# Two mixer stacks on one core: softmax sums spread by TensorE, convolution taps moved later, rotations issued inside a projection

## The chip, the core and the metric

The kernel runs on one core of one Trainium2 chip. The metric is the device time of one execution in microseconds; it is read as the median of several runs. All rows are from one profiled execution of the kernel before.

## What is computed

Input x has 256 positions of 1024 features. The first stack has two layers; each is an RMS norm, a projection `w_in` to 14 groups of 256 columns, four branches, and a projection `w_out` added to x. Two branches are attentions over 4 heads of 64: a sliding window with a sink logit (c) and a neighbourhood attention with a learned bias (d). Each needs

```
p = softmax(scores)           # per head and query, 256 keys
y = (p @ v) * silu(z)         # z: the branch's gate
```

Branch a is a 31-tap depthwise convolution, then a layer norm and SiLU; branch b a gated 3-tap convolution. The second stack has two layers of feed-forward, mixer, feed-forward; its mixer has two causal attentions, one of them (dilated, `dq`, `dk`, `dv`) with a partial rotary embedding of q and k, and a gated linear recurrence computed in 7 levels. Everything is float32. Weights and activations are split into a rounded part and a remainder, so that each product is three matmuls (hi·hi, hi·lo, lo·hi).

## The kernel before

The order of work is written by hand, engine by engine, and tied by semaphores. A mixer is a row of **slots**: slots 0 to 13 are the 14 column groups of `w_in` (orders `ORDER_1`, `ORDER_2`), 14 to 17 the four row groups of `w_out`. A slot is one 1 MB weight tile in a ring of three: SP loads it, ScalarE (ACT) rounds it into `w_hi` (L511), VectorE (DVE) subtracts into `w_lo` (L937), TensorE (PE) multiplies (`project`, 16 steps of 3 matmuls, L1660 to L1662), and DVE or ACT copies the sum out of PSUM (`copy_out`, L990). `project` takes a table `between`: work issued ahead of one of its 16 steps.

An attention is four units (2 branches by 2 blocks of 128 queries). Unit u of the first stack runs so:

- end of PE slot 7+u: `scores` (L1787); DVE in its slot 7+u: `soft` adds the mask or bias and takes the row maximum; ACT: `softmax_exp` with the row sums.
- DVE slot 8+u, first thing: `finish` inverts the sums (L1017) and scales heads 0 and 1 (L1021); ACT slot 8+u: `normalize` scales heads 2 and 3 (L583).
- PE slot 9+u, ahead of step 7 (`TURN_AT`): `turn_probs` transposes the probabilities (L1800), after waiting for both halves of the scaling; ACT copies them to SBUF (`pt_copy`, L613); end of PE slot 9+u: `values` (L1811), then `scores` of unit u+2; DVE: `gated_y` multiplies the result by the gate (L1148).

The second stack's units run the same way, but there ACT scales all heads and `plain_y` takes the result.

DVE also computes the first 20 taps of channel half 0 of the convolution (L1135), in the slots of `DVE_TAPS_AT`; POOL adds the other taps' products, which ACT makes, adds the two parts (L1571), and then does the short convolution of branch b. PE transposes the sum in slot 14 (`conv_to_tm`, L1889), ahead of its second block.

In slots 7 and 8 of the second stack, after the scores, PE multiplies `dq` and `dk` by the rotation matrix into the PSUM tile `aux` (L2036), and DVE's `rotate` (L1031 to L1036) reads it. `aux` is a single tile that the levels of the recurrence (`packed_tile` L1968, read by `take_level` L1357) use too; its users take turns in the order `AUX_ORDER_2`.

```
DVE_TAPS_AT = {2: 3, 3: 3, 4: 2, 5: 2, 6: 2, 8: 2, 9: 2, 10: 2, 11: 2}
TURN_AT = 7
LEVEL_AT = [2 * KT, 2 * KT - 1, 2 * KT - 2, ...]   # level lv goes ahead of step 16-lv of slot 6+lv
```

Of the kernel before, what the change touches and what calls it, by code (L numbers as in the profile page):

```python
# [15 lines left out]
P = 128  # L16
D = 1024
S = 256
# [32 lines left out]
for _i, _n in enumerate(["hq0", "hq1", "hf0", "hf1", "hi0", "hi1", "hg0", "hg1"]):  # L51
# [15 lines left out]
DVE_TAPS_AT = {2: 3, 3: 3, 4: 2, 5: 2, 6: 2, 8: 2, 9: 2, 10: 2, 11: 2}  # L67
# [96 lines left out]
def stacks_kernel(nc, a, out):  # L164

    with ExitStack() as ctx:
# [153 lines left out]
        inv_ready, scaled_dve, scaled_act = sem("inv_ready"), sem("scaled_dve"), sem("scaled_act")  # L320
# [172 lines left out]
        def _(act):  # L493
# [83 lines left out]
            def normalize(un, u, heads, keys=S):  # L577
# [3 lines left out]
                for h in heads:  # L581
                    pr = probs[:, u % 2, h * S:h * S + keys]
                    ins = nc.scalar.activation(pr, pr, ACT.Copy, scale=row_inv[:, c + h:c + h + 1])  # L583
                ins.then_inc(scaled_act, 1)
# [87 lines left out]
            for l in range(DEPTH):  # L672
                base, base3, un = l * LAYER_1, l * (LAYER_1 // RING), l * 4
                gates = 0
                for i, name in enumerate(ORDER_1):
# [5 lines left out]
                    if SC_1 + 1 <= i < SC_1 + 5:  # L681
                        normalize(un, i - SC_1 - 1, (2, 3))
# [20 lines left out]
                    if i == 12:  # L703
# [53 lines left out]
            for l in range(DEPTH):  # L757
# [87 lines left out]
                for i, name in enumerate(ORDER_2):  # L845
# [12 lines left out]
                    if SC_2 + 1 <= i < SC_2 + 5:  # L858
                        normalize(un, i - SC_2 - 1, range(NH), causal_keys(i - SC_2 - 1))
# [58 lines left out]
        def _(dve):  # L918
# [93 lines left out]
            def finish(un, u, has_sink):  # L1012
# [6 lines left out]
                for h in range(2) if un < DEPTH * 4 else ():  # L1019
                    pr = probs[:, u % 2, h * S:(h + 1) * S]  # L1020
                    ins = v.tensor_scalar(pr, pr, row_inv[:, c + h:c + h + 1], None, ALU.mult)  # L1021
                    if h:
                        ins.then_inc(scaled_dve, 1)
# [92 lines left out]
            for l in range(DEPTH):  # L1116
# [25 lines left out]
                def gated_y(u, kt):  # L1142

                    g = proj[:, ix["c_z"] if u < 2 else ix["d_z"], :].rearrange(two, s=S)
                    cols = slice((u % 2) * P, (u % 2 + 1) * P)
                    yv = y_f[:, 0:2 * P].rearrange("p (c s) -> p c s", s=P)
                    dve.wait_ge(mix_written, un + u + 2)
                    v.scalar_tensor_tensor(out=yv, in0=mix[:, 0:2 * P].rearrange("p (c s) -> p c s", s=P), scalar=0.5,  # L1148
                                           in1=g[:, :, cols], op0=ALU.mult, op1=ALU.mult).then_inc(mix_read, 1)
# [4 lines left out]
                for i, name in enumerate(ORDER_1):  # L1154
                    if i == 0:
                        dve.wait_ge(rb_ready, l + 1)
                    if 0 <= i - SC_1 - 1 < 4:
                        finish(un, i - SC_1 - 1, i - SC_1 - 1 < 2)
# [17 lines left out]
                    u = i - SC_1  # L1176
# [937 lines left out]
```

## Time and profile before

| | us |
|---|---|
| median of 3 runs (1280.44 to 1281.99) | 1281.68 |
| the profiled execution, own time | 1284.26 |
| its span in the trace | 1282.4 |
| PE busy / DVE busy / ACT busy / POOL busy | 1261.0 / 987.5 / 705.3 / 262.1 |

The span is the time between the first and the last recorded instruction; the execution's own time has 1.9 us more (1284.26-1282.4). A row of the timeline gives start, duration, engine, line, output<-inputs and count; "[x <-Y]" behind it is idle time just before the row and the work whose end released it. Matmul durations include a drain that overlaps the next matmul, so the pace is read from start to start.

### The profile page before, as it was taken

Reading aid. Unit: us, or ns where it says so; the run is one execution under the profiler, and the core shown is the slowest. Engines: PE = TensorE matmul, PEld = TensorE weight load, DVE = VectorE, ACT = ScalarE, POOL = GpSimd, SP = SyncE. Lnnn points to the kernel's source line nnn. Section 1 sums busy time; section 2 is a strip of 40 time slices with the busy share of each in tenths; the row PEclk is TensorE's granted clock in tenths of the full one; section 3 lists DMA queues with packets and bytes.
Section 4 is the critical chain, followed back from the end, with each engine's and each line's share of the span. In section 5 each row is a group of like instructions: output and inputs, shape, how many; then the busy total and the mean of one; then the engine's idle time right before and its main releaser. Section 6 shows DMA issues by size and latency. Waiting matters only on the chain.

```text
span 1282.4 us, 20996 instructions
## 1 busy us (share of the span) xinstructions
PE 1261.0 (98%) x7922; PEld 1123.4 (88%) x7922; DVE 987.5 (77%) x1195; ACT 705.3 (55%) x945; POOL 262.1 (20%) x258
## 2 busy tenths in 40 slices
PE   9989999999999999999999999999999999999998
PEld 8978998888888899988888888888889998888886
DVE  5998789889766769777776678777676976876676
ACT  5775567465444587736444445444458683644444
POOL 2753164375000023201000009200011320100000
PEclk9999999999999999999999999999999999999999
DMA  8963653556666545346666655766654535666661
GB/s 266 259 186 134 205 157 132 174 171 199 194 196 196 165 133 164 110 128 190 197 197 196 190 170 165 206 188 196 196 158 139 165 107 160 178 197 195 185 187 55
DMA packets 281358, 224.00 MB, mean 175 GB/s; under 512 B 25996, under 2 KB 264234, under 8 KB 281288
## 3 DMA queue, kind: packets, MB, share of 16 engines
q1 hardware_dynamic: 279144, 220.23, 57.1%
q10 hardware_dynamic: 2032, 2.67, 0.7%
q8 instruction: 46, 0.75, 0.3%
q14 instruction: 24, 0.20, 0.0%
q0 software_dynamic: 112, 0.15, 0.0%
HBM read 221.85 MB, written 3.14 MB: 175 GB/s over the span
## 4 chain that ended last, share of the span: by engine, by line
PE 80%; DVE 13%; issue 2%; ACT 2%; DMA 1%; SPq 1%; POOLq 0%; DVEq 0%; POOL 0%; ACTq 0%
PE wide L1693 25%; PE wide L1696 13%; PE big L1660 8%; PE big L1661 8%; PE big L1662 8%; DVE w_lo L937 4%; PE wide L1660 4%; PE wide L1661 4%; PE wide L1662 4%; PE big L1717 1%; DVE work L1135 1%; DVE probs L1000 1%; DMA w_raw<-in_w_in 1%; DVE proj L990 1%; DVE small L1005 1%
## 5 line engine op out<-in xcount | busy, mean ns | idle before, releaser
L937 DVE TENSOR_TENSOR w_lo<-w_raw,w_hi 128x2048 fp32r<-128x2048 f32 x203 | 472.8, 2332 | 96.8 <-ACT w_hi L511 92.3
L511 ACT ACTIVATE w_hi<-w_raw 128x2048 fp32r<-128x2048 f32 x204 | 389.8, 1912 | 163.8 <-PE big L1662 126.5
L1693 PE MATMUL wide<-h_both,w_hi 128*128 128x512 f32 x1408 | 356.7, 393 | 0.0
L1693 PEld LDWEIGHTS wide<-h_both,w_hi 128*128 128x128 f32 x1408 | 254.5, 189 | 48.6 <-DVE h_both L952 2.0
L1660 PE MATMUL wide<-h_both,w_hi 128*128 128x256 f32 x736 | 213.8, 291 | 0.0
L1661 PE MATMUL wide<-h_both,w_hi 128*128 128x256 f32 x736 | 208.1, 283 | 0.0
L1662 PE MATMUL wide<-h_both,w_lo 128*128 128x256 f32 x736 | 208.0, 283 | 0.0
L1696 PEld LDWEIGHTS wide<-h_both,w_lo 128*128 128x128 f32 x1408 | 194.2, 190 | 15.0
L1696 PE MATMUL wide<-h_both,w_lo 128*128 128x256 f32 x1408 | 198.8, 282 | 0.0
L1660 PE MATMUL big<-w_hi,y_hi 128*128 128x512 f32 x480 | 189.1, 394 | 0.0
L1661 PE MATMUL big<-w_lo,y_hi 128*128 128x512 f32 x480 | 187.3, 390 | 0.0
L1662 PE MATMUL big<-w_hi,y_lo 128*128 128x512 f32 x480 | 187.0, 390 | 0.0
L727 ACT ACTIVATE work<-wide 128x512 f32<-128x512 f32 x88 | 52.5, 597 | 234.0 <-PE wide L1696 233.9
L1660 PEld LDWEIGHTS wide<-h_both,w_hi 128*128 128x128 f32 x736 | 140.9, 191 | 5.5 <-issue 4.2
L1661 PEld LDWEIGHTS wide<-h_both,w_hi 128*128 128x128 f32 x736 | 141.0, 192 | 0.6 <-issue 0.5
L1662 PEld LDWEIGHTS wide<-h_both,w_lo 128*128 128x128 f32 x736 | 140.9, 191 | 0.0
L1528 POOL TENSOR_SCALAR small<-small 128x1 f32<-128x1 f32 (+1 forms) x20 | 4.5, 223 | 601.2 <-ACT probs L515 551.2
L1251 DVE TENSOR_TENSOR work<-wide,work 128x512 f32<-128x512 f32 x88 | 60.7, 690 | 85.0 <-ACT work L727 85.0
L1662 PEld LDWEIGHTS big<-w_hi,y_lo 128*128 128x128 f32 x480 | 90.1, 188 | 19.3
L1660 PEld LDWEIGHTS big<-w_hi,y_hi 128*128 128x128 f32 x480 | 90.3, 188 | 17.0
L1661 PEld LDWEIGHTS big<-w_lo,y_hi 128*128 128x128 f32 x480 | 90.4, 188 | 16.6
L1556 POOL TENSOR_TENSOR work<-work,fz 128x256 f32<-128x256 f32 x60 | 64.4, 1073 | 27.1 <-ACT fz L597 23.0
(252 smaller groups left out, 1461.6 us busy)
## 6 DMA issues: line engine op xcount, KB each, us to landing
w_raw<-in_w_in SPq DMA_DIRECT2D x112, 512.0 KB, 4.8
w_raw<-in_ffn_w_gate SPq DMA_DIRECT2D x88, 512.0 KB, 4.0
w_raw<-in_ffn_w_up SPq DMA_DIRECT2D x88, 512.0 KB, 5.2
w_raw<-in_ffn_w_down SPq DMA_DIRECT2D x88, 512.0 KB, 4.2
w_raw<-in_w_out SPq DMA_DIRECT2D x32, 512.0 KB, 4.0
work<-rpb_shifted SPq DMA_DIRECT2D x32, 64.0 KB, 3.3
rpb_shifted<-rpb_rows SPq DMA_DIRECT2D x10, 147.0 KB
x<-in_x SPq DMA_DIRECT2D x2, 512.0 KB, 6.7
```

Source lines behind the costliest of these rows:

```text
L511: nc.scalar.activation(w_hi[:, r, :], w_raw[:, r, :], ACT.Copy).then_inc(hi_ready, 1)
L727: nc.scalar.activation(tmp_cross[parity].rearrange("p (c s) -> p c s", s=S), wide[:, 2 * parity:2 * parity + 2, S:2 * S], ACT.Copy).then_i ...
L937: v.tensor_tensor(w_lo[:, r, :], w_raw[:, r, :], w_hi[:, r, :].bitcast(F32), ALU.subtract).then_inc(lo_ready, 1)
L990: ins = v.tensor_tensor(proj[:, i, :].rearrange(view, s=S), pj[:, i % 2, :].rearrange(view, s=S), row_scale[:].unsqueeze(1).to_broadcast([ ...
L1000: ins = v.scalar_tensor_tensor(out=pr, in0=big[:, 0:2, :].rearrange("p a (h k) -> p (a h) k", k=S)[:, :, 0:keys], scalar=SCALE, in1=bias, ...
L1251: v.tensor_tensor(both, wide[:, 2 * parity:2 * parity + 2, 0:S], tmp_cross[parity].rearrange(view, s=S), ALU.add).then_inc(pj_read[parity], 1)
L1556: g.tensor_tensor(acc, acc, fz[:, n % PROD_RING, :], ALU.add).then_inc(prod_used, 1)
L1660: t_.matmul(o, a_hi, b_hi, start=first, stop=False, skip_group_check=True)
L1661: t_.matmul(o, a_hi, b_lo, start=False, stop=False, skip_group_check=True)
L1662: return t_.matmul(o, a_lo, b_hi, start=False, stop=last, skip_group_check=True)
L1693: t_.matmul(o, hi[:, kt, c], h_both[:, kt].rearrange("p a s -> p (a s)"), start=kt == 0, stop=False, skip_group_check=True)
L1696: ins = t_.matmul(o[:, 0:S], lo[:, kt, c], h_hi[:, kt, :], start=False, stop=kt == KT - 1, skip_group_check=True)
```

## The change

Three edits. In the first stack the probabilities are turned unscaled: `turn_probs` waits for the exponentials only, the scaling on DVE (L1021) and ACT (L583) is gone, and a new `spread_inverse` on PE broadcasts the inverse sums over the 64 rows of each head into `aux`, at the end of slots 9 to 12; `gated_y` multiplies gate by spread sums and then by the values. `finish` goes behind `copy_out` and stands behind that in the same slot. The turn was already inside a projection and stays there.

The six taps that DVE did in slots 8, 9 and 10 go to slot 6 (three taps instead of two), 11 (three instead of two) and 12 (four instead of none); 20 in all as before. ACT makes the short convolution's products one slot earlier (11), and POOL's addition of the two parts goes behind the short convolution's additions.

In the second stack each rotation goes from behind the scores of slot 7 or 8 to ahead of step 4 of slot 8 or 9, and so ahead of that slot's level in the order of `aux`.

```diff
-DVE_TAPS_AT = {2: 3, 3: 3, 4: 2, 5: 2, 6: 2, 8: 2, 9: 2, 10: 2, 11: 2}
+DVE_TAPS_AT = {2: 3, 3: 3, 4: 2, 5: 2, 6: 3, 11: 3, 12: 4}
-AUX_1 = 4
+AUX_1 = 8
 TURN_AT = 7
+ROT_AT = 4
...
-               + [f"{kind}{i}" for i in range(6, 13) for kind in ("level", "turn")
-                  if kind == "level" or i in (7, 8)]
+               + [f"{kind}{i}" for i in range(6, 13) for kind in ("turn", "level")
+                  if kind == "level" or i in (8, 9)]
...
-                    if SC_1 + 1 <= i < SC_1 + 5:
-                        normalize(un, i - SC_1 - 1, (2, 3))
...
-                    if i == 12:
+                    if i == 11:
                         short_products(l)
...
-                for h in range(2) if un < DEPTH * 4 else ():
-                    pr = probs[:, u % 2, h * S:(h + 1) * S]
-                    ins = v.tensor_scalar(pr, pr, row_inv[:, c + h:c + h + 1], None, ALU.mult)
...
+                    dve.wait_ge(aux_written, n + 1)
+                    v.scalar_tensor_tensor(out=scaled_gate, in0=aux[:, 0:2 * P].rearrange("p (c s) -> p c s", s=P), scalar=0.5,
+                                           in1=g[:, :, cols], op0=ALU.mult, op1=ALU.mult).then_inc(aux_read, 1)
+                    dve.wait_ge(aux_read, n + 2)
                     dve.wait_ge(mix_written, un + u + 2)
-                    v.scalar_tensor_tensor(out=yv, in0=mix[:, 0:2 * P].rearrange("p (c s) -> p c s", s=P), scalar=0.5,
-                                           in1=g[:, :, cols], op0=ALU.mult, op1=ALU.mult).then_inc(mix_read, 1)
+                    v.tensor_tensor(yv, mix[:, 0:2 * P].rearrange("p (c s) -> p c s", s=P), scaled_gate, ALU.mult
+                                    ).then_inc(mix_read, 1)
...
+            def spread_inverse(n, u, order=HORDER):
+                pe.wait_ge(inv_ready, n + 1)
+                for c in range(2):
+                    for low in range(2):
+                        at = 4 * (u % 2) + order[2 * c + low]
+                        ins = t_.matmul(aux[low * HD:(low + 1) * HD, c * P:(c + 1) * P],
+                                        row_inv[:, at:at + 1].to_broadcast([P, HD]), ident, start=True, stop=True,
+                                        skip_group_check=True)
+                ins.then_inc(aux_written, 1)
...
+                    if 0 <= u - 2 < 4:
+                        aux_free()
+                        spread_inverse(l * 4 + u - 2, u - 2, PLAIN if u - 2 < 2 else HORDER)
...
+                    if i in (8, 9):
+                        between[ROT_AT] = rotation
```

PE, first stack, end of slot 9 of layer 0, before (L1811 are the values of unit 0, L1787 the scores of unit 2, L1660 begins slot 10):

```order
L1811 MATMUL wide<-pT,proj 64x128 [waits mix_read,pt_read,cv_ready]
L1811 MATMUL wide<-pT,proj 64x128 x7
L1787 MATMUL big<-proj 128x256 [waits sc_read]
L1787 MATMUL big<-proj 128x256 x3
L1660 MATMUL wide<-h_both,w_hi 128x256 [waits pj_read_even,lo_ready]
```

and with the change (line numbers of the changed file):

```order
L1811 MATMUL wide<-pT,proj 64x128 [waits mix_read,pt_read,cv_ready]
L1811 MATMUL wide<-pT,proj 64x128 x7
L1786 MATMUL big<-proj 128x256 [waits sc_read]
L1786 MATMUL big<-proj 128x256 x3
L1820 MATMUL wide<-cst,small 64x128 [waits inv_ready,aux_read]
L1820 MATMUL wide<-cst,small 64x128 x3
L1659 MATMUL wide<-h_both,w_hi 128x256 [waits pj_read_even,lo_ready]
```

Four matmuls (L1820) stand ahead of the next projection, with a wait for `finish` and one for the tile `aux`.

DVE, first stack, slot 12 of layer 0, before:

```order
L990 TENSOR_TENSOR proj<-wide,row_scale 128x512 [waits slot_done]
L1148 SCALAR_TENSOR_TENSOR y_f<-wide,proj 128x256 [waits mix_written]
L944 CAST y_hi<-y_f 128x2x128 [waits mix_read]
L945 TENSOR_TENSOR y_lo<-y_f,y_hi 128x2x128 [waits dve_chain]
L937 TENSOR_TENSOR w_lo<-w_raw,w_hi 128x2048 [waits hi_ready,yd_ready]
```

and with the change:

```order
L989 TENSOR_TENSOR proj<-wide,row_scale 128x512 [waits slot_done]
L1144 SCALAR_TENSOR_TENSOR tmp<-wide,proj 128x256 [waits aux_written]
L1148 TENSOR_TENSOR y_f<-wide,tmp 128x256 [waits mix_written,aux_read]
L943 CAST y_hi<-y_f 128x2x128 [waits mix_read]
L944 TENSOR_TENSOR y_lo<-y_f,y_hi 128x2x128 [waits dve_chain]
L1129 SCALAR_TENSOR_TENSOR work<-work,parA_all 128x256 [waits yd_ready]
L1129 SCALAR_TENSOR_TENSOR work<-work,parA_all 128x256 [waits dve_chain] x3
L936 TENSOR_TENSOR w_lo<-w_raw,w_hi 128x2048 [waits dve_chain,hi_ready]
```

The gate is multiplied in two steps, and the last four taps (L1129) now stand here, ahead of the remainder of slot 15's weights.

PE, second stack, end of slot 7 of the first mixer, before (L2036 is the rotation of `dq`):

```order
L1787 MATMUL big<-proj 128x128 [waits sc_read,foxc_ready]
L1787 MATMUL big<-proj 128x128 x3
L1790 MATMUL big<-y_lo,y_hi 128x128 x4
L2036 MATMUL wide<-proj,cst 128x256 [waits pj_read_even,aux_read]
L2036 MATMUL wide<-proj,cst 128x256
L1660 MATMUL wide<-w_hi,h_both 128x256 [waits pj_read_even,lo_ready]
```

and with the change:

```order
L1786 MATMUL big<-proj 128x128 [waits sc_read,foxc_ready]
L1786 MATMUL big<-proj 128x128 x3
L1789 MATMUL big<-y_lo,y_hi 128x128 x4
L1659 MATMUL wide<-w_hi,h_both 128x256 [waits pj_read_even,lo_ready]
...
L1661 MATMUL wide<-w_hi,h_both 128x256
L2020 MATMUL wide<-proj,cst 128x256 [waits pj_read_even,aux_read]
L2020 MATMUL wide<-proj,cst 128x256
L1659 MATMUL wide<-w_hi,h_both 128x256
```

Twelve matmuls of slot 8 (left out here but for the first and the last) now run ahead of the rotation and of its wait for `aux`.

## Rows read from the trace of the kernel before

**Rows 1.** The page: busy times; the chain that ended last, by engine.
```profile
PE 1261.0 (98%) x7922; PEld 1123.4 (88%) x7922; DVE 987.5 (77%) x1195; ACT 705.3 (55%) x945; POOL 262.1 (20%) x258
...
PE 80%; DVE 13%; issue 2%; ACT 2%; DMA 1%; SPq 1%; POOLq 0%; DVEq 0%; POOL 0%; ACTq 0%
```

**Rows 2.** The waits of PE over the span: us in total, times, longest.
```profile
PE big L1800 <- ACT probs L583: 9.6, 8, 2.9
PE wide L2036 <- DVE at_x L1357: 3.3, 4, 1.2
```

**Rows 3.** Busy time by stretch: slots 9 and 10, first layer; first number the length.
```profile
67.50:79.50 12.00, 9.10 (x81) 8.22 (x81) 11.60 (x14) 8.14 (x20) 8.01 (x8) 1.00 0.79 229
79.50:89.40 9.90, 9.08 (x82) 8.20 (x80) 9.48 (x15) 6.68 (x15) 3.35 (x5) 1.00 0.59 199
```

**Rows 4.** Timeline of PE: slot 9 of layer 0.
```profile
73.15 1.09 PE L1800 MATMUL big<-cst,probs 128*128 128x128 f32 x8 [2.90 <-ACT probs L583]
74.00 0.36 PE L1660 MATMUL wide<-h_both,w_hi 128*128 128x256 f32 x1
...
77.39 1.09 PE L1811 MATMUL wide<-pT,proj 128*64 128x128 f32 x16
78.42 1.14 PE L1787 MATMUL big<-proj 64*128 64x256 f32 x8
```

**Rows 5.** Timeline, slots 6 to 9 of layer 0; last row slot 7 of layer 1.
```profile
58.74 1.82 DVE L1135 SCALAR_TENSOR_TENSOR work<-work,parA_all 128x256 f32<-128x256 f32 x2
...
64.57 5.58 DVE L937 TENSOR_TENSOR w_lo<-w_raw,w_hi 128x2048 fp32r<-128x2048 f32 x2
...
71.32 0.56 DVE L1016 TENSOR_TENSOR small<-small 128x4 f32<-128x4 f32 x1
...
72.78 0.68 DVE L990 TENSOR_TENSOR proj<-wide,row_scale 128x512 f32<-128x512 f32 x1
...
67.47 0.39 PE L1660 MATMUL wide<-h_both,w_hi 128*128 128x256 f32 x1
...
74.83 1.00 ACT L613 ACTIVATE pT<-big 128x1024 f32<-128x1024 f32 x1
...
186.25 0.69 DVE L990 TENSOR_TENSOR proj<-wide,row_scale 128x512 f32<-128x512 f32 x1 [2.39 <-PE wide L1662]
```

**Rows 6.** Timeline of PE: inverse roots spread over 128 rows, and the matmul behind.
```profile
146.58 0.60 PE L1725 MATMUL big<-cst,small 128*128 128x128 f32 x4
146.94 0.36 PE L1660 MATMUL wide<-h_both,w_hi 128*128 128x256 f32 x1
```

**Rows 7.** Timeline, layer 0, slots 11 to 14: DVE, POOL, PE.
```profile
103.66 1.01 DVE L1135 SCALAR_TENSOR_TENSOR work<-work,parA_all 128x256 f32<-128x256 f32 x2
...
107.62 0.41 DVE L1148 SCALAR_TENSOR_TENSOR y_f<-wide,proj 128x256 f32<-128x256 f32 x1
108.06 1.03 DVE L944 CAST y_hi<-y_f 128x256 fp32r<-128x256 f32 x1
...
104.89 2.81 POOL L1571 TENSOR_TENSOR work<-work,part_sum 128x256 f32<-128x256 f32 x1 [7.49 <-DVEq L1191]
...
110.04 5.23 POOL L1556 TENSOR_TENSOR proj<-proj,fz 128x256 f32<-128x256 f32 x4 [1.09 <-ACT fz L597]
...
106.45 1.09 PE L1811 MATMUL wide<-pT,proj 128*64 128x128 f32 x16
...
114.72 0.60 PE L1889 MATMUL wide<-cst,work 128*128 128x128 f32 x4
```

**Rows 8.** Timeline, second stack, first mixer, slots 8 and 9: PE, then DVE.
```profile
513.67 1.13 PE L2036 MATMUL wide<-proj,cst 128*128 128x256 f32 x4 [1.22 <-DVE at_x L1357]
514.45 0.47 PE L1660 MATMUL wide<-w_hi,h_both 128*128 128x256 f32 x1
...
507.61 0.68 DVE L1031 TENSOR_TENSOR tmp<-wide,sin 128x512 f32<-128x512 f32 x1
...
512.89 0.73 DVE L1357 COPY_PREDICATED at_x<-masks,wide 128x512 f32<-128x512 uint8 x1
```

More of the change, by code:

```diff
@@ L575, in softmax_exp, with normalize @@
                 ins.then_inc(probs_exp, 1)
-            def normalize(un, u, heads, keys=S):
+            def normalize(un, u, keys):
                 act.wait_ge(inv_ready, un + u + 1)
                 c = 4 * (u % 2)
-                for h in heads:
+                for h in range(NH):
                     pr = probs[:, u % 2, h * S:h * S + keys]
                     ins = nc.scalar.activation(pr, pr, ACT.Copy, scale=row_inv[:, c + h:c + h + 1])
-                ins.then_inc(scaled_act, 1)
+                ins.then_inc(probs_scaled, 1)
             def tap_products(l, k0, k1):
@@ L858, in _ @@
                     if SC_2 + 1 <= i < SC_2 + 5:
-                        normalize(un, i - SC_2 - 1, range(NH), causal_keys(i - SC_2 - 1))
+                        normalize(un, i - SC_2 - 1, causal_keys(i - SC_2 - 1))
                     if i != 3:
@@ L1176, in _ @@
                     u = i - SC_1
+                    if 0 <= u - 1 < 4:
+                        finish(un, u - 1, u - 1 < 2)
                     if 0 <= u < 4:
@@ L1455, in _ @@
                         q = proj[:, ix["dq" if i == 7 else "dk"], :]
-                        rotate(ax2 + AUX_IX_2[f"turn{i}"], q, cos2[:], sin2[:], 2, q)
+                        rotate(ax2 + AUX_IX_2[f"turn{i + 1}"], q, cos2[:], sin2[:], 2, q)
                     if 0 <= u - 2 < 4:
@@ L1568, in _ @@
                     add_product(l * PRODS + k - 1, conv_acc[:, c] if c else part)
-                pool.wait_ge(conv_part, l + 1)
-                pool.sem_inc(pool_step, 1)
-                g.tensor_tensor(conv_acc[:, 0], conv_acc[:, 0], part, ALU.add).then_inc(conv_ready, 1)
                 two = "p (c s) -> p c s"
@@ L1583, in _ @@
                         add_product(l * PRODS + TAP_PRODS + 2 * c + j - 1, cbx[:, c])
+                pool.wait_ge(conv_part, l + 1)
+                pool.sem_inc(pool_step, 1)
+                g.tensor_tensor(conv_acc[:, 0], conv_acc[:, 0], part, ALU.add).then_inc(conv_ready, 1)
                 pool.wait_ge(*evacuated(l * NPROJ + ORDER_1.index("b_b")))
@@ L1794, in turn_probs @@
             def turn_probs(n, u, keys=S):
-                pe.wait_ge(scaled_act, n + 1)
                 if n < DEPTH * 4:
-                    pe.wait_ge(scaled_dve, n + 1)
+                    pe.wait_ge(probs_exp, n + 1)
+                else:
+                    pe.wait_ge(probs_scaled, n - DEPTH * 4 + 1)
                 pe.wait_ge(pt_read, n + 1)
@@ L1997, in _, with turn_unit, rotation @@
                         between = {FLIP_AT: turn_second, CROSS_AT: cross} if pl == LEVELS else {}
+                    def turn_unit():
+                        turn_probs(l * 4 + 8 + i - SC_2 - 2, i - SC_2 - 2, causal_keys(i - SC_2 - 2))
+                    def rotation():
+                        aux_free(f"turn{i}")
+                        src = ix["dq" if i == 8 else "dk"]
+                        pe.wait_ge(*evacuated(mq + src))
+                        for c in range(2):
+                            ins = t_.matmul(aux[:, c * S:(c + 1) * S], rot2, proj[:, src, c * S:(c + 1) * S],
+                                            start=True, stop=True)
+                        ins.then_inc(aux_written, 1)
+                    if i in (8, 9):
+                        between[ROT_AT] = rotation
                     if 0 <= i - SC_2 - 2 < 4:
-                        between[TURN_AT] = lambda: turn_probs(l * 4 + 8 + i - SC_2 - 2, i - SC_2 - 2, causal_keys(i - SC_2 - 2))
+                        between[TURN_AT] = turn_unit
                     if i >= 2:
@@ L2030, in _ @@
                                    causal_keys(u))
-                    if i in (7, 8):
-                        aux_free(f"turn{i}")
-                        src = ix["dq" if i == 7 else "dk"]
-                        pe.wait_ge(*evacuated(mq + src))
-                        for c in range(2):
-                            ins = t_.matmul(aux[:, c * S:(c + 1) * S], rot2, proj[:, src, c * S:(c + 1) * S],
-                                            start=True, stop=True)
-                        ins.then_inc(aux_written, 1)
                 def hgrn_out(t):
```

8 lines of the change are left out of this document (3 added, 5 removed).

## Prediction

> **What bounds the kernel now.** I read the page's busy times and the chain that ended last first: PE is busy for 98% of the span and holds 80% of the chain [rows 1]. So work that leaves DVE or ACT is worth nothing by itself; only PE's own work and PE's waits count. The view of PE's waits names them. The turns of the first stack wait 9.6 us in eight places for the scaled probabilities, the longest 2.9; the rotations of the second stack wait 3.3 us in four places for a level to be read out of the shared tile, the longest 1.2 [rows 2]. The rest of PE's waits stand at the start of the kernel. Third, the stretches: in slot 9 of layer 0 DVE is busy 11.60 of 12.00 us, in slot 10 9.48 of 9.90, while PE's own work is 9.1 in both [rows 3]. Here alone DVE sets the pace, and PE's waits are what is left over. Fourth, the timeline, to see what each wait would meet next.
>
> Changes within 0.2% (2.6 us) count as no change here, about what a measurement can tell.
>
> **Turns without the scaling.** The eight waits go if nothing else is late. The turn then needs the exponentials, which the slot before has finished: for unit 0 they are followed only by the scaling that leaves. Gain 9.6 us. The scaling itself (two operations on DVE, two on ACT per unit) runs beside PE and counts nothing once the wait is gone; the second step in `gated_y` adds one operation like the 0.41 us one [rows 7] in its place, also beside PE.
>
> **The spread of the sums.** Per unit four matmuls of 128 columns with 64-wide weights, all on PE's path. The nearest row has this shape: the values are eight such matmuls, recorded as 16, and take 78.42-77.39 = 1.03 us from start to start [rows 4], so four take 0.51. The other near row spreads inverse roots by the same trick, but over 128 rows: two matmuls take 146.94-146.58 = 0.36 us [rows 6], so four would take 0.72. I take 0.51, since halves of 64 rows alternate as in the values; 8 x 0.51 = 4.1 us, bounds 4.1 and 5.8. This is a cost on the very engine that bounds. The Trainium skill ("FP8 and Floating Point Precision", TensorE Precision Notes) says that true FP32 goes through the array in four passes; by that alone a unit would cost 4 x 4 x 128 columns at 2.4 GHz, an estimate of 0.85 us, or 6.8 us in all. The values are the same kind of matmul at 0.13 us each [rows 4], less than the 0.21 of four passes, so the rule and the trace differ, and the row decides for the cheaper price.
> Its waits: the inverse sums come out of DVE a slot earlier, right behind `copy_out`. For unit 0 `copy_out` ends at 72.9 (below), the inverse some 0.8 us later, and PE wants them behind the values and the scores, at 77.4. The tile was read in the slot before. No wait.
>
> **One more tap in slot 6.** In layer 0 DVE runs without a gap from the two taps at 58.74 to the double remainder at 64.57, whose first half ends at 64.57+5.58/2 = 67.4; PE starts slot 9, which needs it, at 67.47 [rows 5]. A third tap (1.82/2 = 0.91) makes this start 0.9 us later, at 68.4. In layer 1 DVE idles 2.39 us before its slot 7 [rows 5], and the tap is free. Cost 0.9 us. What is late next is ACT's copy of the turned probabilities, which stands behind a tanh that waits for DVE's `copy_out` of slot 8. That moves by +0.91 for the tap and by 72.78-71.32 = 1.46 the other way, since `finish` and the scaling no longer stand ahead of it; the copy ends at 74.83+1.00-0.55 = 75.3 [rows 5]. PE reaches the values 21 matmuls of (77.39-74.00)/27 = 0.126 and then 77.39-73.15 = 4.24 us [rows 4] after 68.4, at 75.3. They meet; 0.1 us at most.
>
> **Taps out of slots 8 to 10.** Two taps take 1.8 us [rows 5]. With them and the scaling (0.6) gone and one operation of 0.41 [rows 7] added, DVE's slot 10 falls from 9.48 [rows 3] to 7.5, below PE's 9.1+0.5 with the spread. This is what keeps the waits from coming back elsewhere.
>
> **Last taps in slot 12.** PE's `conv_to_tm` needs POOL's final addition. Now that is ready 7 us before it is wanted (104.89+2.81 against 114.72) [rows 7]. With the change DVE does `gated_y` behind the spread of slot 12 (2.2 us: two operations of 0.41, the cast and a remainder, with the links between), then four taps at 0.5 (1.01/2) = 2.0, then POOL 0.1+2.8, because a weight remainder starts beside it as now. That is 7.2 us after the spread; PE gets from the start of slot 13 (106.45+1.03) to `conv_to_tm` in 114.72-107.48 = 7.2 us [rows 4, 7]. They meet as well. Each layer: 0.15 us; bounds 0, if the addition takes the 1.1 us of an undisturbed one, and 1.6, if the taps go at 0.91 [rows 5]. POOL's short additions, now ahead, take 5.2 us and start one slot (9 us) before 110.04 [rows 7], so they end some 2 us before the last tap. Cost 0.3 us.
>
> **Rotations inside the projection.** The wait at 513.67 ends with DVE's reading of the level, 512.89+0.73 = 513.62 [rows 8]. DVE has no gap in this stretch, so it does not get earlier. PE does: without this wait and the first rotation's (3.3/2-1.22 = 0.4) it starts slot 9 at 513.67-1.22-0.4 = 512.0 and reaches step 4, twelve matmuls on, at 513.4, so some 0.25 us of wait are left. In slot 8 the level now follows the rotation in the tile: DVE reads the rotation by 507.61+0.68 = 508.3 [rows 8], PE wants the tile at 508.5. It just passes. Against this, leaving a projection once more costs: behind scores, the next projection's second matmul is 0.1 us late. Gain per mixer 3.3/2-0.25-2x0.1 = 1.2 us, in all 2.4; bounds 0 and 3.3. DVE's `rotate` waits for PE now, but PE passes step 4 before DVE is through `soft`, so DVE stands still for nobody. Behind `rotate` wait the next `finish` and remainder; two slots of slack.
>
> **Sum.** -9.6+4.1+0.9+0.3 = -4.3 in the first stack, -2.4 in the second: 6.7 us less. The profiled execution's own 1284.26 would become 1277.6; it stands 2.6 above the median of the runs, 1281.68, so for the median I say 1281.68-6.7 = **1275.0**.
>
> **Rivals.**
> 1. *The convolution tail binds.* If the last taps take 0.9 each, PE waits 1.6 in each layer, 3.2 instead of 0.3: 1277.9. For it: taps do cost that while POOL works [rows 5]. Against: POOL should be idle by then.
> 2. *The spread does not run in pairs.* At 0.72 each 1.7 us more, 1276.7. For it: the rows of the other spread. Against: its weights are 128 wide, these are 64. By the four passes that the Trainium skill names, full and one after another, it would be 1277.7 (an estimate).
> 3. *Rotations keep their wait.* PE meets DVE at the tile a little further on (at level 8, where I have 0.2 us of margin), and the second stack gives nothing: 1277.4.
> 4. *The first stack gives nothing back.* PE's waits move from the turn to the values, which need ACT's copy; DVE, not PE, still paces slots 9 to 12. Then only the second stack gains: about 1279.5, no change.
> 5. *Slower.* The spread is a new wait on PE, in order ahead of every projection, and `gated_y` must have read the tile and the values before the next ones. If DVE's slot took over 1.2 us more than PE's 9.6, that is 10.8, PE would lose 1.2 us at each of eight spreads, 9.6 in all, against 6.7: 1284.6. For it: the cast in `gated_y` takes 1.03 instead of 0.3 us when POOL works beside it [rows 7], and one operation was added. Against: I count 7.5 us for DVE's slot, so 3.3 would have to come from somewhere. That decides against it.
> That the change does not do what it says can be excluded: the order of instructions shows each move.
>
> **Chances.** Forecast 0.56, rival 1 0.12, rival 2 0.08, rival 3 0.12, rival 4 0.08, slower 0.04. Rivals 1 to 3 are still faster by over 2.6 us: faster 0.87, same 0.09, slower 0.04 ("same" is rival 4 and 0.01 for rivals 1 and 3 together). The range: at best every wait goes, 9.6+3.3-4.1 = 8.8 us, which gives 1272.9; less half the spread of the runs shown (0.8) and something for waits that cost more than their idle time: 1271.5. At the other end rivals 1 to 3 and part of rival 4: 1279.5.
>
> **What would show it.** In the profile after: no wait of PE before the turns, or under 0.3 us; eight records per spread, 0.51 us from start to start; slot 9 of layer 0 starting at 68.3 instead of 67.5; `conv_to_tm` starting within 0.5 us of the end of POOL's addition, with a wait of PE under 0.4; one wait of about 0.25 us before the second rotation of each mixer. A wait of PE before L1811, before L1820 or before the projections of slots 10 to 13 would make the prediction wrong, as would taps of 0.9 us in slot 12.

## The result and the profile after

| | before | changed |
|---|---|---|
| median of 4 runs each (lowest to highest) | 1281.12 us (1280.44 to 1281.99) | **1272.19 us** (1271.64 to 1273.19) |
| ratio (95% interval) | 1 | 0.993 (0.9914 to 0.9945), 8.9 us less |
| span of the profiled execution | 1282.4 | 1269.8 |

Three more comparisons of the changed kernel, made beside the experiments below, gave 1272.52, 1271.69 and 1272.02 us, ratios 0.9926, 0.9925 and 0.993. So the change is worth 9 to 10 us. ("us less" is worked out from the ratio here and below, so it can differ by some tenths from the difference of two medians.) The forecast was 6.7 us less (1275.0); the time lies in its range, 2.8 us below the number.

The page of the changed kernel, its busy times and the chain that ended last, beside [rows 1]:

```profile
PE 1260.5 (99%) x7986; PEld 1124.0 (89%) x7986; DVE 986.7 (78%) x1187; ACT 697.5 (55%) x929; POOL 270.0 (21%) x258
...
PE 90%; DVE 6%; ACT 2%; issue 2%; DMA 0%; POOLq 0%; SPq 0%; DVEq 0%; POOL 0%; ACTq 0%
```

PE's busy time is about the same, 1260.5 against 1261.0 us, although 64 records were added: the profiled execution of before also has two stretches in which PE ran at half its pace (below), so this line does not show what the spread costs. PE's share of the chain rose from 80% to 90%, DVE's fell from 13% to 6%. The waits of PE, whole list, in the columns of [rows 2]:

```profile
PE wide L1832 <- DVE kc L1036: 1.5, 1, 1.5
PE big L1716 <- DMA x<-in_x: 1.1, 1, 1.1
PE wide L1659 <- DVE h_both L951: 0.3, 1, 0.3
```

All three stand in the first 10 us. No turn and no rotation has a mark of idle time any more; both rows of [rows 2] are gone. PE in slots 9 and 10 of layer 0, the answer to [rows 4]; unit 2, without scores behind its values, stands under the first dots:

```profile
73.00 1.09 PE L1811 MATMUL wide<-pT,proj 128*64 128x128 f32 x16
74.03 1.13 PE L1786 MATMUL big<-proj 64*128 64x256 f32 x8
75.09 0.66 PE L1820 MATMUL wide<-cst,small 128*64 128x128 f32 x8
75.68 0.38 PE L1659 MATMUL wide<-h_both,w_hi 128*128 128x256 f32 x1
...
91.98 1.09 PE L1811 MATMUL wide<-pT,proj 128*64 128x128 f32 x16
92.90 0.61 PE L1820 MATMUL wide<-cst,small 128*64 128x128 f32 x8
93.44 0.39 PE L1659 MATMUL wide<-h_both,w_hi 128*128 128x256 f32 x1
```

The spread L1820 takes 0.59 us from start to start behind scores and 0.54 behind values. The values in front of it give some back when the spread follows them: 92.90-91.98 = 0.92 instead of 1.03. So it adds 0.59 in units 0 and 1 and 0.43 in units 2 and 3, 4.1 us over the kernel.

The same two slots by stretch, in the columns of [rows 3]:

```profile
66.20:75.68 9.48, 9.48 (x90) 8.63 (x89) 9.09 (x10) 6.72 (x18) 7.67 (x7) 1.00 0.96 282
75.68:85.17 9.49, 9.49 (x91) 8.64 (x89) 9.01 (x12) 8.40 (x16) 4.83 (x6) 1.00 0.63 215
```

PE is busy from end to end. A slot takes 9.48 us where it took 12.0 and 9.9. DVE, the third pair, still has 9.0 of 9.5 us of work, not the 7.5 that I had counted.

**One yardstick for all kernels.** The inverse-root spread (L1725 before, L1724 after, [rows 6]) opens each stage of a layer. From its first start to its second is layer 0 of the first stack with its FFN, to its third is layer 1; the fourth to the fifth and the seventh to the eighth hold one mixer of the second stack each. The start-up and what happens elsewhere drop out of these differences (us):

| kernel | layer 0 | layer 1 | mixer 1 | mixer 2 |
|---|---|---|---|---|
| before | 126.74 | 125.03 | 136.00 | 137.48 |
| changed | 122.46 | 122.35 | 134.56 | 134.51 |
| e1 rotations only | 125.53 | 125.06 | 134.54 | 134.50 |
| e2 taps only | 124.09 | 123.87 | 135.99 | 135.92 |
| e3 spread only | 122.70 | 122.70 | 136.00 | 137.46 |
| e4 early finish, no spread | 125.06 | 123.41 | 134.59 | 134.51 |
| e5 spread and rotations | 122.47 | 122.68 | 134.58 | 134.50 |
| e6 spread twice | 123.94 | 124.16 | 134.62 | 134.51 |
| e7 six taps in slot 6 | 123.78 | 122.36 | 134.61 | 134.52 |
| e9 wide spread | 126.98 | 130.45 | 134.58 | 134.47 |
| e11 wide copy | 123.80 | 124.20 | 134.55 | 134.48 |

The differences between before and changed are 4.28, 2.68, 1.44 and 2.97, in all 11.4 us. Another 1.2 lie at the start, so the spans differ by 12.6, more than the medians' 8.9. Three parts of that belong to the one profiled execution of before. At the start the same eight transposes took longer in it (before, then changed), and its matmuls kept that slower pace until 10.5 us, though the profile gives a granted clock of 1.00 there:

```profile
6.92 1.94 PE L1717 MATMUL big<-cst,x 128*128 128x128 f32 x8 [0.81 <-DMA x<-in_x]
...
6.81 1.07 PE L1716 MATMUL big<-cst,x 128*128 128x128 f32 x8 [1.09 <-DMA x<-in_x]
```

Its layer 0 is 1.2 us longer than that of e1, which runs the same first stack. And the 1.5 us more in its mixer 2 are lost clock: behind the wait of the second rotation, whose row in mixer 1 [rows 8] has 1.13 us of busy time, PE was granted half its clock, 1.2 instead of 2.4 GHz. The rotation, then the stretch behind it (granted clock: third number from the end):

```profile
1020.32 1.76 PE L2036 MATMUL wide<-proj,cst 128*128 128x256 f32 x4 [1.20 <-DVE at_x L1357]
...
1020.80:1024.10 3.30, 3.30 (x15) 3.03 (x14) 3.26 (x6) 0.43 (x1) 0.00 (x0) 0.50 0.94 294
```

Matmuls of 256 columns start every 0.21 us there instead of every 0.12. e3, with its rotations unchanged, shows the same behind its wait of 1.21 (137.46, granted clock 0.50 from 1013.4 to 1016.6 us); e2, with the same wait of 1.22, does not. The changed kernel has no such stretch before its last few microseconds in any of its four profiles. Against e1 for the first stack and e2 for the mixers, the change gives 3.07+2.71+1.43+1.41 = 8.6 us, near the medians' 8.9. Lost clock also spreads the runs of before: of those made beside the experiments the two slowest, 1285.07 and 1284.89 us, had mean granted clocks of 0.994 and 0.995, the two at 1.000 took 1280.67 and 1280.66, and all of the change's lie at 0.999 or 1.000.

### The profile page after: what moved, and what is told of

It reads as the page before. It is cut to its first block, busy times and chain, and to the rows that moved or that the text cites. A ratio compares the mean times of both kernels' runs of the same rounds, so it can differ in the third digit from the quotient of the medians.

```text
span 1269.8 us, 21116 instructions
## 1 busy us (share of the span) xinstructions
PE 1260.5 (99%) x7986; PEld 1124.0 (89%) x7986; DVE 986.7 (78%) x1187; ACT 697.5 (55%) x929; POOL 270.0 (21%) x258
## 4 chain that ended last, share of the span: by engine, by line
PE 90%; DVE 6%; ACT 2%; issue 2%; DMA 0%; POOLq 0%; SPq 0%; DVEq 0%; POOL 0%; ACTq 0%
PE wide L1692 26%; PE wide L1695 13%; PE big L1659 9%; PE big L1660 9%; PE big L1661 8%; PE wide L1659 6%; PE wide L1660 6%; PE wide L1661 6%; DVE w_lo L936 2%; PE wide L1811 1%; PE big L1716 1%; PE big L1800 1%; PE big L1786 1%; DVE work L1345 1%; PE wide L1981 1%
## 5 line engine op out<-in xcount | busy, mean ns | idle before, releaser
L1660 PE MATMUL wide<-h_both,w_hi 128*128 128x256 f32 x736 | 208.1, 283 | 0.0
L1660 PE MATMUL big<-w_lo,y_hi 128*128 128x512 f32 x480 | 187.3, 390 | 0.0
L1660 PEld LDWEIGHTS wide<-h_both,w_hi 128*128 128x128 f32 x736 | 141.0, 192 | 0.5 <-issue 0.5
L1660 PEld LDWEIGHTS big<-w_lo,y_hi 128*128 128x128 f32 x480 | 90.4, 188 | 16.6
```

What stands on the lines that cost most here:

```text
L1660: t_.matmul(o, a_hi, b_lo, start=False, stop=False, skip_group_check=True)
```

## Experiments

Every kernel ran beside the kernel before on the same chip. "Change" is the changed kernel, and lines of edits are named as in the diff.

**The parts apart: e1, e2, e3.** e1 takes the hunks on the rotations alone (`AUX_ORDER_2`, `ROT_AT`, `rotation()`, `turn{i + 1}`); e3 those on the sums' path (`AUX_1`, the semaphores, `normalize`, `finish`, `gated_y`, `turn_probs`, `spread_inverse`); e2 the taps and what goes with them, POOL's last addition moved behind its short ones and:

```diff
-DVE_TAPS_AT = {2: 3, 3: 3, 4: 2, 5: 2, 6: 2, 8: 2, 9: 2, 10: 2, 11: 2}
+DVE_TAPS_AT = {2: 3, 3: 3, 4: 2, 5: 2, 6: 3, 11: 3, 12: 4}
-                    if i == 12:
+                    if i == 11:
                         short_products(l)
```

> Only the rotations go inside the projections of slots 8 and 9; the first stack stays as before. My theory (each edit takes away its own wait of PE, and the three add up): 2 x 1.42 us, as the two traces show it for the first mixer, so 2.8 us less than the kernel before, and no wait of PE before the rotations. Rival (PE meets DVE at the shared tile a little later, and the gain of the whole change came from the first stack): within 1 us of before, with a wait before the level or the second rotation.

Measured: 1278.03 us against 1281.74, ratio 0.9973 (0.9961 to 0.9984), 3.5 us less. The yardstick says 1.4 us per mixer.

> Only the taps of slots 8 to 10 move to slots 6, 11 and 12, with POOL's final addition behind the short convolution; the scaling of the probabilities stays and nothing is spread. Theory A (the scaling is what PE waits for, so only the spread takes the waits away): the eight waits before the turns stay within 1 us of their 9.6 in sum, time within 1 us of before. Theory B (DVE's queue is what makes the scaling late, and the taps are what fills it): the waits of units 1 to 3 go, six of eight, and only those of unit 0 in either layer stay, some 1.8 us each; 5 to 6 us less than before without any spread.

Measured: 1279.04 us, ratio 0.9976 (0.9966 to 0.9985), 3.1 us less. PE's waits outside the start:

```profile
PE big L1799 <- ACT probs L583: 4.0, 2, 2.2
PE wide L2035 <- DVE at_x L1357: 3.3, 4, 1.2
PE wide L1888 <- POOL work L1582: 1.1, 1, 1.1
```

Six of the eight waits before the turns are gone though the scaling is still there: the scaling of units 1 to 3 was late because it queued behind the taps of the slot before. That of unit 0 stands behind the double remainder (5.58 us, [rows 5]), and its turn waits on, in each layer. The late taps bring one wait of 1.1 us before the convolution's projection, in layer 1. In layer 0 the granted clock fell behind the wait of 2.20 (0.57 over the stretch 72 to 76 us). That cost PE some 1.5 us, an estimate from the half-speed part, and brought it to this place 0.14 us behind the end of POOL's addition.

> Only the spread of the sums, the turn of unscaled probabilities and the two-step gate; the taps stay in slots 8 to 11 and the rotations where they were. Theory A: all eight waits go, the spreads cost 4.1 us, 5 to 6 us less than before. Theory B: the turns wait no more, but with 9.3 us of work in a slot DVE now barely keeps up with PE's 9.6, so some of the wait comes back before the values or the projections, 0 to 1 us each in slots 10 to 12: 2 to 5 us less than before.

Measured: 1276.56 us, ratio 0.9956 (0.9943 to 0.9969), 5.6 us less. The taps are where they were, yet the eight waits are gone. What is left of them:

```profile
PE wide L1811 <- DVE y_f L1147: 0.5, 2, 0.3
```

Either move alone removes most of the same waits, so their gains can't be added.

**e4: can the wait go without the spread?** The taps and the rotations of the change, the scaling kept, and `finish(0)` drawn into slot 7 behind the remainder that PE needs first:

```diff
+                    if 1 <= i - SC_1 - 1 < 4:
+                        finish(un, i - SC_1 - 1, i - SC_1 - 1 < 2)
...
+                        finish(un, 0, True)
```

> Taps and rotations as in the change, but no spread: the probabilities are scaled as before, and the finish of unit 0 goes from the start of DVE's slot 8 to its slot 7, between the two weight remainders. Theory B: with the taps gone from slots 8 to 10 units 1 to 3 wait no more, and the earlier finish takes the 3 us that unit 0 was late, so all waits go without the 4.1 us of the spreads: 11 to 12.5 us less than before, 2 to 4 us less than the whole change. Theory A: the scaling stays late for units 1 to 3, their waits stay at some 5.8 us in sum, and this is slower than the whole change by 1 us or more.

Measured: 1274.57 us, ratio 0.9942 (0.9929 to 0.9955), 7.4 us less, slower than the change by 1.5 to 2.2 between the ratios; each of its runs (1274.24 to 1275.32) is above each of the change's 19 (1271.56 to 1273.19), though none of those was made beside it. The turns of unit 1 wait in both layers, that of unit 2 in one, the values of unit 0 and the convolution's projection in both:

```profile
PE big L1801 <- ACT probs L584: 2.5, 3, 1.0
PE wide L1890 <- POOL work L1584: 2.1, 2, 1.1
PE wide L1812 <- issue: 1.2, 2, 0.9
```

The turn of unit 0 no longer waits, but the early `finish` moves DVE's second remainder and `copy_out` back, behind them ACT's tanh and its copy of the turned probabilities; that ends at 74.30, and the values start at 74.40 after 0.88 us of idle time. The expectation that this would beat the change fell: 4.1 us of matmuls are cheaper than the 6.2 us of waits in this version (the rows above and 0.4 before slot 9). Only 2.5 of these stand before the turns. The 2.1 at the convolution are there because PE, without the spreads, comes earlier to taps that end late. By the yardstick layer 0 is 2.6 us over the change and layer 1 is 1.1; DVE was late in layer 0 of this execution and not in layer 1 (see the tap in slot 6 below). A version without the spread and with the last taps earlier than slot 12 was not tried, so it is not shown that the spread is the cheapest way.

**e5: are the taps needed?** The change with `DVE_TAPS_AT`, `short_products` and POOL's addition as before.

> The spread and the moved rotations, with the convolution taps of the first stack where they were before. Theory A (by the time the scale has left VectorE's chain, the taps' places matter little): the two changes add, -5.4 and -3.7 us against the kernel before, so -8.5 to -9.5, about the whole change (1272.2 us), with two waits of some 0.3 us before the values of slot 10 in place of 0.24 us before the projection behind the convolution. Theory B (the tap move is a part of the gain in its own right, as the run of the taps alone with -3 us suggests): 2 to 3 us slower than the whole change, so 1274 to 1275.

Measured: 1273.4 us, ratio 0.9931 (0.9918 to 0.9945); the change on the same chip (e8) 1272.52. The intervals overlap, and the yardstick gives 0.3 us between them (0.01+0.33). Its one row of waits beyond the start:

```profile
PE wide L1812 <- DVE y_f L1148: 0.5, 2, 0.2
```

So theory A holds: once the scaling is out of DVE's line, the move of the taps is worth 0.3 us by the trace, and not over 1 by the medians. It swaps two small waits before the values for one of 0.24 before the convolution's projection (below).

> The changed kernel itself, on the same chip as the three others, for the differences between them: 1271.6 to 1273.2 us, as in the comparison with the kernel before, and by every theory -8 to -9.5 against it.

Measured: 1272.52 us, ratio 0.9926 (0.9913 to 0.994).

**e6: what does the spread cost?**

```diff
-                for c in range(2):
+                for c in (0, 1, 0, 1):
                     for low in range(2):
```

> The whole change with each of the eight spreads issued twice (the second pair of matmuls writes the same sums again), so that the price of a spread is measured by itself. Theory A (the spread stands fully on TensorE's path): eight times 0.51 us, so +4.1 us over the whole change, 1276 to 1277. Theory B (part of it fills time in which TensorE would wait, or the pitch of 0.13 us a matmul is not what it costs): +0 to +2 us, or at four passes of 0.21 us a matmul +6.8.

Measured: 1275.11 us, ratio 0.9947 (0.9933 to 0.996), 2.6 us over e8; the spans are 3.5 apart, 1273.3 and 1269.8. One of the eight:

```profile
75.17 1.09 PE L1820 MATMUL wide<-cst,small 128*64 128x128 f32 x16
76.20 0.39 PE L1659 MATMUL wide<-h_both,w_hi 128*128 128x256 f32 x1
```

1.03 us against 0.59: four more matmuls cost 0.44, and nothing hides them. The other 0.15 of the first four are the price of leaving the projection behind scores. The expected 4.1 was 0.51 eight times; the trace has 0.44 eight times.

**e7: what does DVE have to spare in slot 6?**

```diff
-DVE_TAPS_AT = {2: 3, 3: 3, 4: 2, 5: 2, 6: 3, 11: 3, 12: 4}
+DVE_TAPS_AT = {2: 3, 3: 3, 4: 2, 5: 2, 6: 6, 11: 3, 12: 1}
```

> The whole change with three of slot 12's four taps moved on into slot 6, which then has six instead of three. It doubles the cost that the prediction put at 0.9 us for a single tap there, which no row of the change shows. Theory A (slot 6 has some 1.2 to 1.5 us to spare on VectorE): three taps of 0.91 us are 2.7 us, so a wait of TensorE of 1.2 to 1.6 us in layer 0 and 0 to 1.2 in layer 1, less 0.24 us before the projection behind the convolution: +1 to +2 us over the whole change. Theory B (slot 6 has nothing to spare, as the prediction had it): +2.7 in each layer that is late, up to +5.

Measured: 1274.88 us, ratio 0.995 (0.9937 to 0.9964), 2.4 us over e8 with a wide spread of its runs (1273.18 to 1277.8); by the yardstick, read from the fastest of them, 1.3, all in layer 0. The first cost of 2.7 us of taps is where the prediction had put a single one, before slot 9 of layer 0, and a second follows before the values:

```profile
67.26 0.39 PE L1659 MATMUL wide<-h_both,w_hi 128*128 128x256 f32 x1 [0.89 <-DVE w_lo L936]
84.22 1.09 PE L1811 MATMUL wide<-pT,proj 128*64 128x128 f32 x16 [0.39 <-DVE y_f L1148]
```

Layer 1 takes all three taps for nothing. The yardstick's 1.3 lies in Theory A's +1 to +2 and the medians' 2.4 above it, both far from Theory B's 5; the wait of 0.89 is less than its 1.2 to 1.6.

**e9: a cheaper spread.** DVE writes each inverse 64 times over, and one matmul with a full-width stationary replaces two of 64:

```diff
-                link(v.reciprocal(row_inv[:, c:c + 4], row_sum[:, c:c + 4]))
+                    link(v.reciprocal(inv_wide[:, u % 2, :].rearrange("p (a b d) -> p a b d", a=2, b=2),
+                                      src.unsqueeze(3).to_broadcast([P, 2, 2, HD])))
...
+                    ins = t_.matmul(aux[:, c * P:(c + 1) * P], inv_wide[:, u % 2, c * P:(c + 1) * P], ident,
+                                    start=True, stop=True, skip_group_check=True)
```

> The whole change with the spread in two matmuls of a full 128-column stationary instead of four of 64: VectorE writes the inverse sums 64 times over, in the order of the heads (256 elements a partition instead of 4), and one matmul per group of channels turns them. In the run with the spread issued twice the four added matmuls took 0.44 us, 0.11 each. Theory A (a matmul costs its pass over the 128 moving columns, whatever its stationary): eight times 0.22, so -1.8 us against the change, 1270.5 to 1271.2, and no new wait, since the reciprocal's added 0.3 to 0.5 us lies in VectorE's slack. Theory B (the wider stationary takes as long as the two narrow ones together, or the longer reciprocal delays the values): 0 to +1 us against the change.

Measured: 1286.23 us, ratio 1.0037 (1.0023 to 1.0051): slower than before the change, and 14.5 us over e10. A clear miss, and the most telling run. DVE first, then PE's waits:

```profile
70.65 1.75 DVE L1021 RECIPROCAL inv_wide<-small 128x256 f32<-128x256 f32 x1
```
```profile
PE wide L1905 <- POOL work L1588: 4.6, 2, 3.8
PE wide L1817 <- DVE y_f L1154: 4.2, 2, 2.5
```

A reciprocal of 256 elements takes 1.75 us where I had counted 0.5. The Trainium skill ("VectorE: DVE Perf Modes", First, the fixed hardware budget) says that it runs as an iterative divide with a repeat count of 8; the trace agrees in kind, a copy of as many elements takes 0.29 (e11). These 1.6 us per unit come back as 8.8 us of waits, and the waits cost clock. The stretches after the wait of 2.5 and after the one of 3.8, the granted clock being the third number from the end:

```profile
84.00:92.00 8.00, 6.96 (x52) 6.08 (x53) 7.58 (x10) 4.68 (x11) 2.06 (x3) 0.79 0.36 122
92.00:100.00 8.00, 8.00 (x76) 7.70 (x75) 7.72 (x9) 5.59 (x12) 4.75 (x3) 1.00 0.23 70
...
240.00:250.00 10.00, 8.41 (x28) 6.93 (x29) 8.57 (x13) 1.67 (x2) 4.02 (x4) 0.66 0.40 110
```

Full speed is 1.00, so parts of these stretches ran at 1.2 instead of 2.4 GHz: the granted clock was 0.51 from 86.5 to 90.0 us, with PE busy throughout, and 0.51 from 240 to 247, with PE busy for 5.4 us. The layers are 4.5 and 8.1 us longer than the change's; PE's waits cover 3.2 and 5.5 of it, and half of those 3.5 and 5.4 us of slow work, an estimate of 1.7 and 2.7, about the rest. The length of the wait alone doesn't decide: the 1.72 us in layer 1 here and the 2.90 in layer 0 of before [rows 4] cost no clock, the 1.20 in mixer 2 of before did.

The matmuls themselves:

```profile
75.23 0.71 PE L1824 MATMUL wide<-cst,inv_wide 128*128 128x128 f32 x4
75.70 0.36 PE L1665 MATMUL wide<-h_both,w_hi 128*128 128x256 f32 x1
```

0.47 us against 0.59: only 0.12 less for half the matmuls. Theory A's price was wrong: a matmul of 64-wide weights is not as dear as a full one.

> The changed kernel itself, on the same chip as the wide spread, for the difference between the two: 1271.6 to 1273.2 us by every theory.

Measured: 1271.69 us, ratio 0.9925 (0.9911 to 0.9938).

**e11: the same with a cheap DVE part.** The reciprocal of 4 elements stays, and a copy widens it:

```diff
+                    link(v.tensor_copy(inv_wide[:, u % 2, :].rearrange("p (a b d) -> p a b d", a=2, b=2),
+                                      src.unsqueeze(3).to_broadcast([P, 2, 2, HD])))
```

> The wide spread with the reciprocal of 4 elements kept and a copy behind it that writes each inverse sum 64 times over (256 elements; copies and multiplications of 256 elements took 0.3 to 0.4 us). In the run of the wide reciprocal the spread's start to the next matmul's was 0.47 us against the change's 0.59, 0.12 less, and the loss came from VectorE: 1.75 us for a reciprocal of 256 elements. Theory A (VectorE's 1.6 us of added reciprocal was the whole loss): with 0.5 us added instead of 1.6, no wait of a microsecond, and -0.5 to -1 us against the change by eight times 0.12, so 1271 to 1272. Theory B (VectorE has no half microsecond to spare between the turn and the values): waits before the values and before the convolution's projection of 0.2 to 0.6 us each, +1 to +2 us against the change.

> The changed kernel itself once more, on the same chip as the wide copy: 1271.6 to 1273.2 us by every theory.

Measured: 1276.12 us, ratio 0.9959 (0.9945 to 0.9973), and the change beside it (e12) 1272.02, ratio 0.993 (0.9916 to 0.9943). So 4.1 us over the change, by the yardstick 3.2. Theory B, at twice its price:

```profile
70.07 0.29 DVE L1020 COPY inv_wide<-small 128x256 f32<-128x256 f32 x1
```
```profile
PE wide L1904 <- POOL work L1587: 2.8, 2, 1.4
PE wide L1816 <- DVE y_f L1153: 0.7, 2, 0.4
```

A copy of 0.3 to 0.5 us per unit on an engine that is busy for 78% of the span turns a saving of 1 us on PE into a loss of 3 to 4. None of the versions tried beats the change.

## Why the prediction was right, and where it was off

**Turn waits, predicted -9.6.** They are gone, but they were worth more than their marks. Take the first stack of e1, 250.59 us, and of the change, 244.81: 5.8 less. e1's eight marks sum to 8.4 us, 4.1 are spent on the spread and 0.24 at the convolution. 5.8+4.1+0.24 = 10.1 us must have gone with eight waits, so each cost 0.2 us more than its mark. The rows show where. Around unit 0's turn, e1 and then the change:

```profile
68.83 0.28 PE L1663 MATMUL wide<-h_both,w_lo 128*128 128x256 f32 x1
70.88 1.09 PE L1801 MATMUL big<-cst,probs 128*128 128x128 f32 x8 [1.77 <-ACT probs L584]
71.73 0.36 PE L1661 MATMUL wide<-h_both,w_hi 128*128 128x256 f32 x1
...
68.69 0.28 PE L1661 MATMUL wide<-h_both,w_lo 128*128 128x256 f32 x1
68.81 1.03 PE L1800 MATMUL big<-cst,probs 128*128 128x128 f32 x8
69.61 0.36 PE L1659 MATMUL wide<-h_both,w_hi 128*128 128x256 f32 x1
```

A mark counts from the modelled end of the last matmul, whose record is 0.28 us long where the next one follows 0.12 us later; that hides 0.16. And the turn itself takes 0.85 us to the next start behind a wait, 0.80 without: 0.05 more. The step that failed is the sum of idle marks taken as the price, 1.6 us too low. The range had allowed for it ("waits that cost more than their idle time"), the number had not.

**The spread, predicted +4.1.** 0.59 us in four units and 0.43 in the other four instead of 0.51 in each, sum 4.1. That the two cases average to the 0.51 is luck; the size was right, and e6 shows that it stands fully on PE's path. The explanation was incomplete. I held 0.13 us a matmul against the rule of four passes in the Trainium skill ("FP8 and Floating Point Precision", TensorE Precision Notes) and said that they differ. By e6 a pair of 64-wide matmuls adds 0.22 us, and four passes over 128 columns at 2.4 GHz are an estimate of 0.21. So what I took for a cheap matmul is a pair sharing the time of one. Full-width matmuls have that price: two took 0.47 in e9, and the two of a rotation, with 256 columns each, put 0.87 us between their neighbours (495.65 to 496.76, less the usual 0.24), 0.22 per 128 columns. The Trainium skill has this too ("TensorEngine Tiling (Array Packing)", Key Properties: different tiles can run their matmuls in parallel), and the trace agrees. The price was read off the right row, since that row had the same pairs.

**A tap in slot 6, predicted +0.9.** It cost nothing. DVE in slots 6 and 7 of layer 0, answering [rows 5]:

```profile
55.36 2.73 DVE L1129 SCALAR_TENSOR_TENSOR work<-work,parA_all 128x256 f32<-128x256 f32 x3
58.32 0.69 DVE L989 TENSOR_TENSOR proj<-wide,row_scale 128x512 f32<-128x512 f32 x1 [0.24 <-PE wide L1661]
...
62.15 5.57 DVE L936 TENSOR_TENSOR w_lo<-w_raw,w_hi 128x2048 fp32r<-128x2048 f32 x2
```

Behind three taps DVE waits for PE for 0.24 us, and the first half of the double remainder ends at 62.15+5.57/2 = 64.9, 1.3 before PE wants it at 66.2. In the execution that I read, DVE was late in this place. Its double remainder starts 44.73 us behind the yardstick's first row in layer 0 and 43.50 behind the second in layer 1; in layer 0 of the changed kernel's four profiles, of e1, e5 and e6 it is 43.50. In layer 0 of e4 its first half starts at 45.13. What makes DVE late stays open. e1, with the same first stack, had 1.77 before its first turn instead of 2.90. The step took a lateness of one profiled execution for a property of the kernel. With six taps the mechanism appears just where it was forecast (e7).

**DVE's slots and the taps out of 8 to 10.** "This is what keeps the waits from coming back elsewhere" was wrong twice. e5 leaves the taps in these slots and loses 0.3 us. And DVE's slot is not 7.5 of 9.6 us but 9.0 of 9.5: the stretch ([rows 3] answered above) also holds work left over from the slot before, and single operations were longer than counted: a remainder took 2.83 us there and 2.29 one slot later, the cast of `y` 0.73 and 0.29. What decides is how far DVE is ahead at the point where PE needs it. The reading of unit 0's values by `gated_y`:

```profile
81.46 0.42 DVE L1148 TENSOR_TENSOR y_f<-wide,tmp 128x256 f32<-128x256 f32 x1
```

It ends at 81.88, and PE writes unit 1's into the tile from 82.49: 0.6 us of margin. One slot later it is 1.9 (89.69+0.42 against 91.98). This 0.6 is what e5, e7, e9 and e11 used up, each with its first wait on `y_f` here; so did e3.

**Convolution tail, predicted +0.3.** DVE, POOL and PE in layer 0, answering [rows 7]:

```profile
103.95 2.05 DVE L1129 SCALAR_TENSOR_TENSOR work<-work,parA_all 128x256 f32<-128x256 f32 x4
...
106.22 2.82 POOL L1582 TENSOR_TENSOR work<-work,part_sum 128x256 f32<-128x256 f32 x1 [2.59 <-DVEq L1191]
...
109.18 0.63 PE L1902 MATMUL wide<-cst,work 128*128 128x128 f32 x4
```

Taps at 0.5 us, POOL's addition at 2.8, as predicted, and PE starts 0.14 behind its end, 0.24 late; in layer 1 it isn't late. This is the place with the least margin, and rival 1 is the one that e11 (1.4 us per layer) and e4 (1.1) called up.

**Rotations, predicted -2.4.** 1.43 us per mixer instead of 1.2, 2.9 in all; e1 alone gives the same. The wait before the second rotation, predicted at 0.25, is there, although no mark shows it. Mixer 1, the first rotation, which starts 0.12 us behind the start of the matmul ahead of it, and then that matmul and the rotation for the second:

```profile
495.77 1.03 PE L2020 MATMUL wide<-proj,cst 128*128 128x256 f32 x4
...
505.16 0.28 PE L1661 MATMUL wide<-w_hi,h_both 128*128 128x256 f32 x1
505.51 1.13 PE L2020 MATMUL wide<-proj,cst 128*128 128x256 f32 x4
```
```profile
504.72 0.74 DVE L1357 COPY_PREDICATED at_x<-masks,wide 128x512 f32<-128x512 uint8 x1
```

The second starts 0.35 us behind the one ahead of it instead of 0.12, and 0.05 behind the end of DVE's reading (504.72+0.74 = 505.46). It does so in both mixers of all four profiles of the change, by 0.33 to 0.35, and takes 0.10 longer to the next start: a price of 0.33 in mixer 1 for a wait that I had at 0.25. So the residual was forecast rightly. The gain is larger for the reason of the first step: the removed waits, too, cost 0.1 to 0.2 us more than their marks. Before, the second rotation started 1.95 us behind the group ahead of it (511.72 to 513.67), where with the change the projection starts 0.66 behind the same group (503.09 to 503.75): 1.29 for a mark of 1.22 (an estimate, since different matmuls follow), and again 0.10 more to the next start. Lost clock behind such a wait, 1.5 us in mixer 2 of before, comes on top in some executions and is not in these 2.9.

**Rivals.** None came true in the change. The chance of faster, 0.87, stood on rivals 1 to 3 being faster still. Rival 5 was closer than I judged: I had 3.3 us to spare on DVE, the margin was 0.6 us, and e9 with 1.6 more per unit ended on the other side.

The sum by what was measured: first stack -8.4-1.6+4.1+0.2 = -5.7, rotations -2.9, together -8.6 instead of -6.7. Of the 1.9 between them 0.4 is the net of the first step (10.0 for 9.6), 0.9 the tap, 0.1 the convolution, 0.5 the rotations.

## What to carry to other kernels

Where PE fills the span, moving 4 us of work onto it can pay if it takes the end of a chain through two other engines out of PE's path; price a wait as its mark plus 0.2 us, and look at the granted clock behind it. Don't read an engine's slack from its busy share (78% here, and 0.3 us more per unit already cost 3): read the gap between the end of its reading and the start of PE's writing at each meeting, and take the smallest. Check a lateness of one execution against a second place or layer before it goes into the sum.

## What was not expected of the hardware

- Two matmuls with 64-wide weights on the two halves of the output run in the time of one: 0.22 us a pair (e6), 0.47 for two full-width ones with the return to the projection (e9).
- A reciprocal of 256 elements took 1.75 us and one of 4 took 0.18, a copy of 256 took 0.29 to 0.51.
- A wait of PE can cost clock besides. In or behind waits of 1.20 us (before, mixer 2), 1.21 (e3, mixer 2), 2.20 (e2), 2.45 and 3.82 (e9) stretches of 3 to 7 us ran at a granted clock of 0.50 to 0.57; behind 1.22 (before, mixer 1), 1.72 (e9) and 2.90 (before, layer 0) none did. In an otherwise busy stretch the fall cost about 1.5 us.
- A row of PE can start late without a mark of idle time: 0.35 instead of 0.12 us behind the row ahead (second rotation of the change).
- The first matmuls of before and e2 ran at half the pace until about 10.5 us, where the profile gives a granted clock of 1.00. This was not resolved.
